# Layer one of a two-block network on Trainium2: 32x32 products apart from each other, ScalarE's U0 copy and the last pair's order moved

## The chip, the cores and the metric

The kernel runs on one core of one Trainium2 chip. A core has TensorE (PE in the profile, its weight loads are PEld), VectorE (DVE), ScalarE (ACT), GpSimd (POOL) and SyncE (SP), which here only issues DMAs. The metric is the device time of one execution in microseconds (us). It is read as the median of three runs.

## The reference

The program is a stack of four layers on 512 tokens of width 1024, each with a norm ahead and a residual sum behind. Layer one is the one that is changed. Its input projection gives nine parts; the part that matters here is a recurrent state per head:

```
z = h @ even_w_in[j]
a_val, a_glu, a_gate, r, k, v, wd, ad, b_gate = split_cols(z, EVEN_SIZES)
ya = conformer_conv(a_val, a_glu, ...) * silu(a_gate)      # 31 taps over time, per channel
yb = rwkv7_mix(r, k, v, wd, ad, ...) * silu(b_gate)
out = concatenate([ya, yb]) @ even_w_out[j]

def rwkv7_step(state, inp):            # 16 heads of 64, scanned over 512 tokens
    r_t, w_t, k_t, v_t, kk_t, a_t = inp
    sa = einsum('bhvk,bhk->bhv', state, -kk_t)
    state = state * w_t + sa[..., None] * (kk_t * a_t) + v_t[..., None] * k_t
    y = einsum('bhvk,bhk->bhv', state, r_t)
```

The other layers (sparse attention, a linear recurrence, attention with forget gates) are computed by code that the change does not touch.

## The kernel before

The 16 heads are worked off in eight pairs; a pair fills the 128 partitions. The scan over tokens is replaced by chunks of 64 tokens: in each chunk a triangular 64x64 system is solved, and a short chain carries the state from chunk to chunk. All eight chunks and both heads of a pair are handled at once.

To invert the triangular matrices, the kernel works on their 32x32 diagonal blocks with products of 32x32 matrices (`quarters`, line 1277; each set has 32 matmuls, which the trace shows as 64 records, for float32 runs in two passes). `sq1`, `sq2`, `sq3` square the matrix again and again; `sq2p`, `sq3p`, `sq4` multiply the powers into the running inverse `inner`; `off0`, `merge0`, `off1` and `merge1` join 16-blocks to 32-blocks and these to 64-blocks. Between two sets ScalarE copies the product out of PSUM (line 1883), VectorE transposes it (line 1647) or adds it to `inner` (line 1652). After `merge1` VectorE copies the result to `PT` (line 1665). Then come 64x64 products: `PAt`, `U0`, `PA`, `G`, `C`. `G` on TensorE needs VectorE's copy of `PAt` (line 1671); the second half of `C` needs ScalarE's copy of `U0` (line 1864). Six `chain` steps, `U`, `Y` and `y` end the pair.

The projections of the next pair are spread between these products. A projection has eight steps, `k0` to `k7`, then `r0` to `r7`, `v`, `glu`, `val`, `gate`. A step is three matmuls of 128x128 by 512 columns (lines 524, 525, 528), since each float32 weight is split into a rounded part `w_hi` (ScalarE, line 480) and a rest `w_lo` (GpSimd, line 498). Each is made in two halves of a block, and a step waits for the half that it reads. There are two split buffers and four raw ones. In them the labels `wk0`, `wk1`, `wr0` and so on are the halves for the block two places further on: `wk0` and `wk1` make v's weights, `wr0` and `wr1` glu's, `wv0` and `wv1` val's.

SyncE fetches the blocks in the order of a plan, each as soon as the block four places ahead of it has left its raw buffer (the loop from `weights_in`, line 441):

```
old = k.plan[n - NRAW] if n >= NRAW else None
free = None if old is None else ("rest_made", old[0], 1) if old[4] else ("modulated", old[0])
for w in need(free):
    e.wait_ge(*w)
e.dma_start(k.raw[n % NRAW][:, 0:kt * width], src)
```

Here NRAW is 4. Blocks of `ada` (for the modulation vectors) are not split; VectorE reads them once, in `ada0` to `ada3` (line 747), and so frees them. For each pair the plan is k, ada0, r, ada1, v, ada2, ada3, glu, val, gate.

VectorE fills its time with the 31 convolution taps of a channel block (`tap0` and so on, line 1599), which depend on nothing in the solve.

The order on each engine is written out by hand in three tables: `FIRST_ORDER` (ahead of and in the first pair), `ORDER` (for pairs in the middle) and `LAST_ORDER`. Every engine's streams are merged by the place of a label in its table. A `'` behind a label means one pair later, a `^` one period later in the first and last tables. Engines are in-order: an instruction that waits holds all that stands behind it.

In the last pair there is no next pair to project; its cover is the rest of the gates (`gate`, `cg`), the convolution norm's sums (`mean`, line 1459) and, on VectorE, the last 31 taps.

Of the kernel before, what the change touches and what calls it, by code (L numbers as in the profile page):

```python
# [3507 lines left out]
```

## Time and profile before

| what | value |
|---|---|
| median of 3 runs | 1765.78 us (1763.6 to 1766.76) |
| the profiled execution, its own time | 1764.11 us |
| span of its trace | 1762.4 us |
| mean granted clock of TensorE | 0.977 |
| PE, DVE, ACT, POOL busy | 1664.6, 1235.5, 806.0, 795.9 us |
| the eight pairs of layer one | about 88 to 620 us of the span |

Busy time is the sum over the whole span. Since the layers have different limits, what a change in the solve is worth is read from the solve's own stretches, engine by engine: a wait ahead of an instruction is shown in square brackets with what released it. The granted clock is in parts of 2.4 GHz; it is either 1.00 (2.4 GHz) or 0.50 (1.2 GHz), and means lie between.

### The profile page before, as it was taken

The numbers are of one execution on the slowest core, as the hardware profiler recorded it, in microseconds if no ns is written. First come the engines' busy times: TensorE is split into PE (matmuls) and PEld (weight loads), VectorE is DVE, ScalarE is ACT, GpSimd is POOL, SyncE is SP. The second block draws the span as 40 slices with busy tenths as digits, with TensorE's granted clock in tenths as the row PEclk, the third lists the DMA queues.
The fourth block names the chain that finished last, engine by engine and source line by source line (L and its number), as shares of the span: only waits on it lengthen the run. The fifth ranks groups of instructions, "written<-read, shape, count | busy, mean of one in ns | idle before, by whom it ended". The sixth has DMA issues, their size and how long they took to land.

```text
span 1762.4 us, 38758 instructions
## 1 busy us (share of the span) xinstructions
PE 1664.6 (94%) x16172; PEld 1267.4 (72%) x16172; DVE 1235.5 (70%) x2231; ACT 806.0 (46%) x1505; POOL 795.9 (45%) x713
## 2 busy tenths in 40 slices
PE   5899999999989899999999999999999999999997
PEld 5677776777776668757777777787777778777766
DVE  7578878988879788269997777535887436355553
ACT  3544444454443273365544444434767433444443
POOL 3534334344342245457883222544545545544433
PEclk9999999999999999999999999999999999999998
DMA  7212311312313123212221111123222232433312
GB/s 305 95 63 74 110 54 70 121 51 74 121 51 133 38 96 125 96 48 73 84 96 49 37 37 37 61 96 108 72 84 71 82 99 81 140 115 117 109 57 90
DMA packets 51902, 155.12 MB, mean 88 GB/s; under 512 B 5888, under 2 KB 12032, under 8 KB 51600
## 3 DMA queue, kind: packets, MB, share of 16 engines
q1 hardware_dynamic: 51728, 152.65, 25.6%
q8 instruction: 128, 2.10, 0.5%
q14 instruction: 46, 0.38, 0.1%
HBM read 150.50 MB, written 2.13 MB: 87 GB/s over the span
## 4 chain that ended last, share of the span: by engine, by line
PE 66%; DVE 20%; ACT 5%; issue 4%; POOL 2%; DVEq 0%; POOLq 0%; ACTq 0%
PE bank L524 16%; PE bank L528 14%; PE bank L525 14%; PE bank L1272 7%; PE bank L2360 3%; DVE ya L1599 2%; DVE best L2468 2%; DVE lru_xc L2852 2%; DVE score L2471 2%; PE bank L3077 1%; PE bank L1230 1%; PE bank L2390 1%; PE bank L3092 1%; DVE probs_t L2515 1%; PE bank L570 1%
## 5 line engine op out<-in xcount | busy, mean ns | idle before, releaser
L498 POOL TENSOR_TENSOR w_lo<-raw,w_hi 128x512 fp32r<-128x512 f32 (+2 forms) x434 | 578.6, 1349 | 603.2 <-ACT w_hi L480 591.7
L524 PE MATMUL bank<-h_hi,w_hi 128*128 128x512 f32 x1368 | 578.1, 423 | 10.2 <-ACT h_hi L973 2.5
L528 PE MATMUL bank<-h_lo,w_hi 128*128 128x512 f32 x1368 | 543.3, 397 | 10.8 <-DVE h_lo L941 6.3
L525 PE MATMUL bank<-h_hi,w_lo 128*128 128x512 f32 x1368 | 541.5, 396 | 0.0
L480 ACT ACTIVATE w_hi<-raw 128x512 fp32r<-128x512 f32 (+2 forms) x434 | 248.1, 603 | 252.7 <-PE bank L528 172.0
L524 PEld LDWEIGHTS bank<-h_hi,w_hi 128*128 128x128 f32 x1368 | 260.9, 191 | 100.2 <-issue 34.0
L528 PEld LDWEIGHTS bank<-h_lo,w_hi 128*128 128x128 f32 x1368 | 260.7, 191 | 77.1 <-DVE h_lo L941 11.4
L525 PEld LDWEIGHTS bank<-h_hi,w_lo 128*128 128x128 f32 x1368 | 261.5, 191 | 57.4 <-issue 9.3
L1599 DVE SCALAR_TENSOR_TENSOR ya<-padded,vecs,ya 128x512 f32<-128x512 f32 x240 | 214.2, 893 | 3.9
L3153 DVE CUSTOM_DVE_ANT_0 fox_probs<-bank,fox_keybias 128x128 f32<-128x128 f32 (+3 forms) x64 | 28.9, 488 | 84.7 <-PE bank L3077 84.4
L524 PE MATMUL bank<-own_hi,w_hi 128*128 128x512 f32 x208 | 82.9, 398 | 1.6 <-ACT own_hi L973 1.6
L528 PE MATMUL bank<-own_lo,w_hi 128*128 128x512 f32 x208 | 82.3, 396 | 0.0
L525 PE MATMUL bank<-own_hi,w_lo 128*128 128x512 f32 x208 | 82.0, 394 | 0.0
L3239 ACT ACTIVATE fox_probs<-fox_probs,fox_small 128x128 f32<-128x128 f32 (+3 forms) x64 | 35.5, 555 | 76.9 <-DVE fox_small L3159 76.9
L2360 PE MATMUL bank<-probs_t,values 32*128 32x256 f32 x1024 | 65.1, 394 | 5.1 <-DVE probs_t L2515 5.1
L2002 POOL TENSOR_TENSOR tables<-shifted_r 128x512 f32<-128x512 f32 x8 | 8.8, 1095 | 127.0 <-PE bank L528 127.0
L2360 PEld LDWEIGHTS bank<-probs_t,values 32*128 32x128 f32 x1024 | 50.7, 189 | 18.6 <-DVE probs_t L2515 8.5
L1883 ACT ACTIVATE W<-bank 128x256 f32<-128x256 f32 x32 | 12.3, 385 | 103.9 <-PE bank L1272 103.9
L1064 DVE SCALAR_TENSOR_TENSOR x<-bank,mod,x 128x512 f32<-128x512 f32 x16 | 12.0, 749 | 68.1 <-PE bank L528 68.1
L2555 ACT ACTIVATE attn_tmp<-bank 64x512 f32<-64x512 f32 (+1 forms) x54 | 31.9, 592 | 52.2 <-PE bank L528 48.7
L1062 DVE TENSOR_TENSOR x<-bank,x 128x512 f32<-128x512 f32 x16 | 11.1, 692 | 63.0 <-PE bank L528 63.0
L792 DVE TENSOR_TENSOR squares<-squares,sq 128x512 f32<-128x512 f32 x37 | 34.4, 942 | 27.1 <-ACT sq L782 26.5
(412 smaller groups left out, 2826.8 us busy)
## 6 DMA issues: line engine op xcount, KB each, us to landing
raw<-even_in SPq DMA_DIRECT2D x57, 512.0 KB, 3.7
raw<-odd_in SPq DMA_DIRECT2D x39, 512.0 KB, 3.2
raw<-ada SPq DMA_DIRECT2D x32, 512.0 KB, 4.0
raw<-fox_in SPq DMA_DIRECT2D x25, 512.0 KB, 3.3
raw<-lru_in SPq DMA_DIRECT2D x24, 512.0 KB, 3.2
ada_first<-ada SPq DMA_DIRECT2D x16, 512.0 KB, 13.7
raw<-even_out SPq DMA_DIRECT2D x16, 512.0 KB, 3.3
raw<-odd_out SPq DMA_DIRECT2D x16, 512.0 KB, 3.3
```

What stands on the lines that cost most here:

```text
L480: e.activation(k.w_hi[s % NSPLIT][:, at], k.raw[n % NRAW][:, at], ACT.Copy).then_inc(*did("rounded", key, half))
L498: e.tensor_tensor(k.w_lo[s % NSPLIT][:, at], k.raw[n % NRAW][:, at], k.w_hi[s % NSPLIT][:, at].bitcast(F32), ALU.subtract).then_inc(*did(" ...
L524: e.matmul(out, hi[:, w], x[i][0], start=start and i == 0, stop=False, skip_group_check=True)
L525: e.matmul(out, lo[:, w], x[i][0], start=False, stop=False, skip_group_check=True)
L528: m = e.matmul(out, hi[:, w], x[i][1], start=False, stop=stop and i == kt - 1, skip_group_check=True)
L1272: return e.matmul(out, lhsT, rhs, start=start, stop=stop, skip_group_check=True)
L1599: e.scalar_tensor_tensor(y, u[:, j:j + T], w(j), y, ALU.mult, ALU.add).then_inc(*did("tapped", q, j))
L2360: m = e.matmul(k.banks[3 + i][:, 0:GROUP * KB], k.values[rows, j, :], k.probs_t[n % 2][rows, j, :, :].rearrange("p a q -> p (a q)"), start ...
L2468: e.max(k.best[:, t - t0, :], k.score[:, t, :]).then_inc(*did("made", "best", t, n))
L2471: e.match_replace(k.score[:, t, :], k.best[:, t - t0, :], k.score[:, t, :], TAKEN).then_inc(*did("made", "taken", t, n))
L2852: e.scalar_tensor_tensor(xc, xp[:, j:j + T], w(j), xc, ALU.mult, ALU.add).then_inc(*did("made", *(("lru_tap", n, j) if j < LTAPS - 1 else ...
L3239: e.activation(prob, prob, ACT.Exp, bias=k.fox_small[:, 3 * i:3 * i + 1], scale=1.0, accum_out=k.fox_small[:, 3 * i + 1:3 * i + 2]).then_i ...
```

## The change

Only the tables change; all instructions are the same ones. In `ORDER`, and alike in `FIRST_ORDER` with `^` behind the labels:

```diff
-        gate7' k7 Z sq1 tK tB sq2 sq2p sq3 sq3p r0 r1 sq4 r2 r3 r4 off0 r5 r6 merge0 kk_sum r7 off1 v0 v1
-        v2 v3 merge1 v4 v5 v6 v7 PAt U0 PA G C glu0 glu1 chain1 ...
+        gate7' k7 Z sq1 tK tB r0 sq2 r1 r2 sq2p r3 sq3 r4 r5 sq3p r6 sq4 r7 v0 off0 v1 v2 merge0 kk_sum v3 off1
+        v4 v5 merge1 v6 v7 PAt U0 PA G C glu0 glu1 chain1 ...
```

VectorE's table in `ORDER` follows: it runs `... sq2 tap5 sq2p k_lerp tap6 sq3p f_out tap7 sq4 turn0 tap8 tap9 merge0 turn1 ada0 tap10 tap11 tap12 merge1 tap13 ada1 tap14 tap15 tap16 PAt ...`. On ScalarE `k_copy` comes ahead of `wk0`, `wk1` behind `sq3`, and `U0` ahead of `wr0 wr1 wv0`; on GpSimd `below` comes ahead of `wk0`. In `LAST_ORDER`:

```diff
-        gate7' gate0 gate1 gate2 gate3 gate4 gate5 gate6 gate7 cg00 sq2 sq2p sq3 sq3p mean2 mean3 mean4 mean5 mean6
-        sq4 cg01 cg02 cg03 cg04 cg05 off0 merge0 off1 cg06 cg07 cg10 ...
+        gate7' gate0 gate1 gate2 gate3 sq2 gate4 sq2p gate5 sq3 gate6 sq3p gate7 cg00 mean2 mean3 mean4 mean5 mean6
+        sq4 cg01 cg02 cg03 off0 cg04 cg05 merge0 cg06 off1 cg07 cg10 ...
-        tV ada0 mm0 mm1 N N_t val_done' tap25' ada1 ada2 ada3 f_norm tap26' tap27' tB tap28' tap29' tap30' sq1
+        tV ada0 mm0 mm1 N N_t val_done' tap25' sq1 tB ada1 ada2 f_norm tap26' tap27' tap28' tap29' tap30' ada3
```

and on ScalarE `gate_done` moves behind `sq3`.

TensorE's own order, in the first pair behind the transposes of K and B; the rows with `W` or `inner` are the sets `sq2` and `sq2p`, the others steps of r:

```order
 L1302 MATMUL bank<-ident,B_63 128x128 x4
+L524 MATMUL bank<-h_hi,w_hi_28 128x512
+L525 MATMUL bank<-h_hi,w_lo_30 128x512
+L528 MATMUL bank<-h_lo,w_hi_28 128x512
 L1272 MATMUL bank<-W_75 32x32 x32
+L524 MATMUL bank<-h_hi,w_hi_28 128x512
+L525 MATMUL bank<-h_hi,w_lo_30 128x512
+L528 MATMUL bank<-h_lo,w_hi_28 128x512
+L524 MATMUL bank<-h_hi,w_hi_28 128x512
+L525 MATMUL bank<-h_hi,w_lo_30 128x512
+L528 MATMUL bank<-h_lo,w_hi_28 128x512
 L1272 MATMUL bank<-inner,W_75 32x32 x32
```

One step now stands ahead of `sq2` and two between `sq2` and `sq2p`, where the sets followed each other.

VectorE's order in the first pair, around `merge1` (the copy to `PT`), `turn1` (the transpose of `inner` to `W_75`), `ada1` (L747 on `raw_24`) and the copy of `PAt` (to `W_77`):

```order
+L1599 SCALAR_TENSOR_TENSOR ya<-padded_87,vecs,ya 128x512 x3
+L1665 COPY PT<-bank 128x8x32
 L1599 SCALAR_TENSOR_TENSOR ya<-padded_87,vecs,ya 128x512
 L747 ISA raw_24,mod_11<-raw_24,silu_c 128x1024
 L747 ISA mod_11 128x1
 L752 TENSOR_TENSOR mod_11<-mod_11,vecs 128x1
-L1647 STREAM_TRANSPOSE W_75<-inner 128x256
-L1599 SCALAR_TENSOR_TENSOR ya<-padded_87,vecs,ya 128x512 x6
-L1665 COPY PT<-bank 128x8x32
-L1599 SCALAR_TENSOR_TENSOR ya<-padded_87,vecs,ya 128x512
+L1599 SCALAR_TENSOR_TENSOR ya<-padded_87,vecs,ya 128x512 x3
 L1671 COPY W_77<-bank 128x512
```

`ada1` stood ahead of `merge1` and now stands behind it, with three taps between it and the copy of `PAt`.

ScalarE's order in the first pair, from the end of `kk_root`; `W_75<-bank` is the copy of `U0`, `w_hi` are the roundings `wr0`, `wr1`, `wv0`:

```order
 L1794 ACTIVATE tables<-tables 128x512
 L1786 ACTIVATE shifted_r<-bank 128x512
+L1864 ACTIVATE W_75<-bank 128x512
 L480 ACTIVATE w_hi_28<-raw_24 128x512 x2
 L480 ACTIVATE w_hi_27<-raw_25 128x512
 L1786 ACTIVATE shifted_v<-bank 128x512
-L1864 ACTIVATE W_75<-bank 128x512
 L1910 ACTIVATE PA<-bank 128x256 x2
```

The copy of `U0` has moved from behind three roundings and `v_copy` to ahead of them.

## Rows read from the trace of the kernel before

**Rows 1.** The head of the page: busy time, share of the span, instructions.
```profile
PE 1664.6 (94%) x16172; PEld 1267.4 (72%) x16172; DVE 1235.5 (70%) x2231; ACT 806.0 (46%) x1505; POOL 795.9 (45%) x713
```
**Rows 2.** Stretches: length, busy PE, PEld, DVE, ACT, POOL; PEclk, DMA share, GB/s.
```profile
161.52:190.01 28.49, 26.27 (x846) 20.84 (x842) 22.41 (x38) 14.60 (x27) 8.82 (x7) 0.94 0.22 77
...
428.55:456.72 28.17, 26.20 (x846) 21.02 (x843) 22.48 (x39) 14.60 (x27) 8.84 (x7) 0.94 0.22 78
493.72:525.54 31.82, 27.33 (x846) 21.57 (x843) 22.39 (x38) 14.61 (x27) 9.23 (x8) 0.89 0.20 69
sum 208.79, PE 187.11 PEld 148.35 DVE 156.21 ACT 102.83 POOL 62.58; mean PE 26.73 PEld 21.19 DVE 22.32 ACT 14.69 POOL 8.94
```
**Rows 3.** Timeline of TensorE in the second pair: start, us, what, wait before.
```profile
163.33 0.71 PE L1272 MATMUL bank<-W 32*32 32x32 f32 x62
163.90 0.73 PE L1272 MATMUL bank<-inner,W 32*32 32x32 f32 x62
166.36 0.41 PE L1272 MATMUL bank<-W 32*32 32x32 f32 x27 [1.73 <-DVE W L1647]
168.43 0.80 PE L524 MATMUL bank<-h_hi,w_hi 128*128 128x512 f32 x1
171.29 0.75 PE L1272 MATMUL bank<-inner,W 32*32 32x32 f32 x64
174.25 0.75 PE L1272 MATMUL bank<-inner,W 32*32 32x32 f32 x64
176.52 0.75 PE L1272 MATMUL bank<-W 32*32 32x32 f32 x64
182.53 0.21 PE L1272 MATMUL bank<-W 32*32 32x32 f32 x1
186.15 1.15 PE L1272 MATMUL bank<-A_t,PT 64*64 64x64 f32 x32
188.47 0.22 PE L1272 MATMUL bank<-B_t,W 64*64 64x64 f32 x1
```
**Rows 4.** Two more stretches, columns as above, for the clock.
```profile
168.00:171.00 3.00, 3.00 (x42) 2.19 (x33) 2.43 (x4) 0.18 (x1) 1.35 (x2) 0.50 0.03 5
592.00:603.00 11.00, 8.50 (x255) 7.30 (x256) 9.54 (x16) 2.28 (x5) 1.28 (x1) 1.00 0.20 68
```
**Rows 5.** Timeline of VectorE in the second pair.
```profile
172.09 0.42 DVE L1652 TENSOR_TENSOR inner<-bank,inner 128x256 f32<-128x256 f32 x1 [0.80 <-PE bank L1272]
...
178.32 1.22 DVE L747 CUSTOM_DVE_ANT_0 raw<-raw,silu_c 128x1024 f32<-128x1024 f32 x1
...
180.02 4.65 DVE L1599 SCALAR_TENSOR_TENSOR ya<-padded,vecs,ya 128x512 f32<-128x512 f32 x6
...
187.35 0.69 DVE L1671 COPY W<-bank 128x512 f32<-128x512 f32 x1 [1.69 <-PE bank L1272]
```
**Rows 6.** Timelines of SyncE, ScalarE and GpSimd: fetches and splits of weights.
```profile
179.58 0.80 SPq L449 DMA_DIRECT2D raw<-even_in  x2
194.73 0.33 SPq L449 DMA_DIRECT2D raw<-even_in  x1
197.99 0.63 ACT L480 ACTIVATE w_hi<-raw 128x512 fp32r<-128x512 f32 x1 [8.03 <-DMA raw<-even_in]
186.09 1.66 ACT L480 ACTIVATE w_hi<-raw 128x512 fp32r<-128x512 f32 x3
187.27 2.96 POOL L498 TENSOR_TENSOR w_lo<-raw,w_hi 128x512 fp32r<-128x512 f32 x2
raw<-even_in SPq DMA_DIRECT2D x57, 512.0 KB, 3.7
```
**Rows 7.** Last pair: timelines of VectorE and TensorE.
```profile
569.41 0.44 DVE L1647 STREAM_TRANSPOSE W<-W 128x256 f32<-128x256 f32 x1
570.00 0.71 PE L1272 MATMUL bank<-W 32*32 32x32 f32 x62 [1.74 <-DVE W L1647]
596.52 0.68 PE L1272 MATMUL bank<-A_t,PT 64*64 64x64 f32 x16 [1.70 <-DVE PT L1665]
```

More of the change, by code:

```diff
@@ L1103 @@
         glu5 glu6 glu7 val0 val1 val2 val3 val4 val5 val6 val7 tA^ mm0^ bonus_sum tV^ k0^ w_up^ k1^ k2^ k3^ k4^ k5^
-        mm1^ N^ k6^ k7^ Z^ sq1^ tK^ tB^ sq2^ sq2p^ sq3^ sq3p^ r0^ r1^ sq4^ r2^ r3^ r4^ off0^ r5^ r6^ merge0^
-        kk_sum^ r7^ off1^ v0^ v1^ v2^ v3^ merge1^ v4^ v5^ v6^ v7^ PAt^ U0^ PA^ G^ C^ glu0^ glu1^ chain1^ glu2^
+        mm1^ N^ k6^ k7^ Z^ sq1^ tK^ tB^ r0^ sq2^ r1^ r2^ sq2p^ r3^ sq3^ r4^ r5^ sq3p^ r6^ sq4^ r7^ v0^ off0^ v1^ v2^
+        merge0^ kk_sum^ v3^ off1^ v4^ v5^ merge1^ v6^ v7^ PAt^ U0^ PA^ G^ C^ glu0^ glu1^ chain1^ glu2^
         chain2^ glu3^ chain3^ glu4^ glu5^ glu6^ glu7^ chain4^ val0^ val1^ chain5^ val2^ val3^ val4^ val5^ val6^
@@ L1109 @@
         cum powers carry k_lerp kk_norm A B r_lerp R rk v_lerp V mm0^ val_done tV^ tap0^ cum^ powers^ mm1^ N^ N_t^
-        carry^ tap1^ tap2^ sq1^ tap3^ tB^ tap4^ sq2^ sq2p^ k_lerp^ sq3p^ tap5^ sq4^ ada0^ tap6^ turn0^ tap7^ tap8^
-        merge0^ tap9^ ada1^ turn1^ tap10^ tap11^ tap12^ tap13^ tap14^ tap15^ merge1^ tap16^ PAt^ tap17^ G^ tap18^ C^
+        carry^ tap1^ tap2^ sq1^ tap3^ tB^ tap4^ sq2^ tap5^ sq2p^ k_lerp^ tap6^ sq3p^ tap7^ sq4^ turn0^ tap8^ tap9^
+        merge0^ turn1^ ada0^ tap10^ tap11^ tap12^ merge1^ tap13^ ada1^ tap14^ tap15^ tap16^ PAt^ tap17^ G^ tap18^ C^
         tap19^ chain1^ chain2^ ada2^ chain3^ kk_norm^ tap20^ ada3^ chain4^ A^ chain5^ B^ r_lerp^ chain6^ R^ U^ rk^
@@ L1128 @@
         mm0 val_done' tV tap0 tap25' cum tap26' tap27' powers tap28' tap29' f_norm mm1 N tap30' N_t carry tap1 tap2
-        sq1 tap3 tB tap4 sq2 sq2p k_lerp sq3p f_out tap5 sq4 ada0 tap6 turn0 tap7 tap8 merge0 tap9 ada1 turn1 tap10
-        tap11 tap12 tap13 tap14 tap15 merge1 tap16 PAt tap17 G tap18 C tap19 chain1 chain2 ada2 chain3 kk_norm tap20
+        sq1 tap3 tB tap4 sq2 tap5 sq2p k_lerp tap6 sq3p f_out tap7 sq4 turn0 tap8 tap9 merge0 turn1 ada0 tap10 tap11
+        tap12 merge1 tap13 ada1 tap14 tap15 tap16 PAt tap17 G tap18 C tap19 chain1 chain2 ada2 chain3 kk_norm tap20
         ada3 chain4 A chain5 B r_lerp chain6 R U rk v_lerp tap21 tap22 tap23 tap24 V""",
     "scalar": """
-        tA wval0' wval1' decay f_square f_log f_root powers wgate0' wgate1' before rate gate_done' N sq1 Z wk0 k_copy wk1 sq2
-        tK sq3 off0 kk_sq off1 kk_root r_copy wr0 wr1 wv0 v_copy U0 PA wv1 wglu0 V glu_done t1 wglu1""",
+        tA wval0' wval1' decay f_square f_log f_root powers wgate0' wgate1' before rate gate_done' N sq1 Z k_copy sq2 wk0
+        tK sq3 wk1 off0 kk_sq off1 kk_root r_copy U0 wr0 wr1 wv0 v_copy PA wv1 wglu0 V glu_done t1 wglu1""",
     "gpsimd": """
-        prior wgate0' inner wgate1' k_diff wk0 below wk1 r_diff wr0 wr1 wv0 wv1 v_diff wglu0 wglu1 wval0
+        prior wgate0' inner wgate1' k_diff below wk0 wk1 r_diff wr0 wr1 wv0 wv1 v_diff wglu0 wglu1 wval0
         wval1"""}
@@ L1156 @@
     "scalar": """
-        tA f_square f_log f_root wval0' wval1' N sq1 wgate0' Z tK wgate1' gate_done' gate_done sq2 sq3 off0 wgate0 wgate1
+        tA f_square f_log f_root wval0' wval1' N sq1 wgate0' Z tK wgate1' gate_done' sq2 sq3 gate_done off0 wgate0 wgate1
         wcg00 off1 cg_done0 wcg01 wcg10 wcg11 U0 PA cg_done1 cg_done2 centre0 centre1 t1 f_square^ centre2 centre3 centre4
```

12 lines of the change are left out of this document (6 added, 6 removed).

## The prediction

> **What bounds the kernel now.** I read the head of the page first. TensorE is busy for 94% of the span, so a gain must come from its idle time or from its clock, and it must reach TensorE [rows 1]. The change touches layer one, where eight head pairs are solved one after the other. For each of the first seven I took the stretch from the start of `sq1` to the first `glu` projection. It holds the same work in every pair and takes 28.17 to 31.82 us, 208.79 us in all seven. VectorE is busy in it for about 22.4 us, ScalarE for 14.6. The granted clock is the one number that separates them: mean 0.94 in three stretches (28.17 to 28.49 us), 0.89 in the other four, of which the longest takes 31.82 us [rows 2].
>
> The timeline of one pair says why. Between `sq2p` and `sq3` TensorE waits 1.73 us for a VectorE transpose. After that the clock is at 0.50, which is 1.2 GHz: the first projection after the sets starts at 168.43 and the next set only at 171.29, 2.86 us for two steps [rows 3, 4]. At 2.4 GHz a set with two steps takes 2.27 us (174.25 to 176.52) and a set with three 2.96 us (171.29 to 174.25). So **a step is 0.69 us, and a set that stands alone costs 0.89 us** with its edges [rows 3]. VectorE has nearly as much work. It waits 0.80 us at `sq4` and 1.69 at `PAt`, and taps fill the rest [rows 5].
>
> **Part one: the sets apart.** One or two r and v steps now stand between `sq2`, `sq2p`, `sq3`, `sq3p`, `sq4`. The copy and the transpose that `sq3` waits for take 0.38 to 0.45 us each, and two steps (1.37 us) and a set cover them; so the 1.73 us goes to nothing, and with it what precedes the low clock. The price is edges: back to back a set takes 0.57 us (163.33 to 163.90), alone 0.89, so three more groups cost about 1.0 us a pair [rows 3].
>
> The Trainium skill, "TensorEngine Tiling (Array Packing)", section Tiling Modes, says that changing the tiling mode drains TensorE. That speaks against every set put between 128-row projections. The trace agrees, and prices the drain together with the edges at the 0.3 us a set that I counted; by the rule alone the change would lose that and no more.
>
> Now the walk of one pair with these prices, from 163.3 where the transposes end. Up to `merge1` stand 14 steps (9.6 us), seven sets (6.2), `kk_sum` and the half set `off1` (about 0.85 each, from the like stretch after 176.52). `merge1` starts at 180.8 and `PAt`, two steps on, at 183.1; before they were at 182.53 and 186.15 [rows 3]. So TensorE is 3.0 us early at `PAt`. Were nothing else in the way, the stretch would shrink to 25.4 us (183.1 + 2.3 to `G` + 1.5 to the first `glu` step, less 161.5).
>
> **Part two: what is late next, VectorE.** The transpose `turn1`, both modulations and the taps change places. Between `merge1` and the copy of `PAt` VectorE used to have one tap; now it has a tap, `ada1` and three taps. The `merge1` copy starts 0.80 us after its set (171.29 to 172.09 shows this delay), at 181.6, and ends at 181.9; tap to 182.6; `ada1`, 1.22 us and 0.1 for its small followers, to 184.0; three taps of 0.78 (4.65 us for six) to 186.3; the copy of `PAt`, 0.69 us, to 187.0 [rows 3, 5]. `G` on TensorE needs it and would be ready at 183.1 + 2.3 = 185.4 (186.15 to 188.47 before). **TensorE waits 1.7 us ahead of G**, and `C` ends at 188.6. Behind the waiting `G` stand `C` and all the `glu` steps.
>
> **Part three: what is late after that, the weight ring.** This is where I put the bound. There are four raw buffers, and SyncE fetches in plan order: `glu`'s block takes the buffer that `ada1`'s block leaves. The trace shows it: `ada1` ends its pass at 179.54, and two even blocks (glu, val) are issued at 179.58 [rows 5, 6]. In the changed order `ada1` ends at 183.9, so `glu`'s block is issued 4.3 us later. From issue to the first rounding takes 3.3 us (194.73 to 197.99) to 3.7 (the page's median for such blocks): 187.4 or so. ScalarE rounds half a block in 0.6, GpSimd takes the rest in 1.3 to 1.7 (2.96 us for two), and each hand-over costs about 0.1 [rows 6]. That is 189.6 to 190.2, and I take 189.97. Before, GpSimd had the first half by about 188.8, out of the way. **So the first glu step starts 28.45 us after `sq1`** (ends 28.1 and 28.7), whatever TensorE gained earlier: 1.3 us of waiting stand behind `C`.
>
> Seven stretches are then 7 x 28.45 = 199.2 us against 208.79: **9.6 us less**. Nearly all of it is in the four pairs that had the clock at 0.89; the three others gain nothing.
>
> `U0` ahead of the roundings: its copy now comes where the roundings began before, at 186.09, and `C` needs it at about 188.0, so it hides; before, it sat behind three roundings (1.66 us) [rows 6]. It delays `glu`'s rounding only if that block had landed, which it has not. The GpSimd move (`below` before `wk0`) touches rows needed 5 us later. I cost both at nothing; with the ring out of the way that copy's 0.5 us or so (a third of 1.66) would show at `glu`.
>
> **The last pair.** VectorE comes to its `sq2` transpose at 569.41 without a wait ahead of it, so it is VectorE that is late, and `sq3` follows at 570.00 after 1.74 us [rows 7]. In the new order TensorE has only ten steps ahead of `sq3` where it had thirteen, and VectorE's `sq1` and `tB` come so early that each must wait for TensorE (I put 2 us on both, the 0.80 us delay above twice and a bit for the tap and copy that were cover). So `sq3` would be ready at about 567 and starts at about 571. The three steps come afterwards, partly in place of waits at `off0` and `merge0`. By this walk `merge0` is 1.7 us later: **plus 1.7 us** (0 to plus 4).
>
> **Sum.** The profiled execution took 1764.11 us (1762.4 of span and 1.7 around it). 1764.1 - 9.6 + 1.7 = 1756.2. The median of the three runs is 1.7 above the profiled one, so I forecast **1758 us**; within this case 1754 to 1762.
>
> **The rivals.**
>
> *A. Neither VectorE nor the ring limits.* VectorE catches up earlier in the pair, or the block lands before it is needed. For it: TensorE alone needs 25.4 us, and VectorE's 22.4 us of work fit into 27. The most that I can see is a stretch of 27.2 us, where `C` ends without the ring. That is 18.4 us less in seven; with the last pair's 1.7 back, 1749 us. Against it: the issue at 179.58 follows `ada1` to 0.1 us, so the ring is real.
>
> *B. The clock falls at the new waits, and the change loses.* Place: the 1.7 us ahead of `G` and the 1.3 us behind `C`, with 1.5 us of 64x64 products between. For it: in the pair of the timeline the clock fell after a wait of 1.73 us amid 32x32 products, and all seven stretches have a mean under 1.00 [rows 2 to 4]. Against it: in the last pair a wait of 1.70 us ahead of 64x64 products left the clock at 1.00 over the whole stretch around it [rows 4, 7]. Price: a mean of 0.94 over 28.17 us is 1.7 us lost; 0.89 over 31.82 us is 3.5 [rows 2]. It decides from about five pairs at 1.7: all seven give 1758 + 11.9 = 1770 us, slower than before; all at 3.5 would be 1782. Two or three pairs give 1762, no change.
>
> *C. The waits only move.* The edges, VectorE and the ring eat everything, with stretches of 29 us or more and a last pair at plus 4: 1764 to 1766 us.
>
> **How the numbers follow.** Forecast 0.45, A 0.15, B 0.28 (half of it in few pairs, half in most), C 0.12. Within 0.2% is 3.5 us, about what a measurement of this kernel can tell: 1762.3 to 1769.3. Faster takes the forecast nearly whole, less its upper edge, and A, with the best of B: 0.57. Same takes C and few pairs of B: 0.24. Slower takes the rest of B and a bad last pair: 0.19. The range from 1748 to 1770 leaves out the tails of A and B.
>
> **What would show it.** In the changed profile: no wait over 0.3 us between `sq1` and `merge1`, clock 1.00 there; `merge1` 19.3 us after `sq1`; a wait of 1 to 2 us ahead of `G` for the VectorE copy (L1671); two fetches issued right after `ada1`, 22.4 us after `sq1`; a wait ahead of the first `glu` step for GpSimd's w_lo (L498); all seven stretches alike. The forecast is wrong if the `glu` step starts without that wait (A), if the seven show clocks under 1.00 between `G` and `glu` (B), or if VectorE runs later than the walk has it ahead of `merge1`.

## The result, and the profile after

The change makes the kernel a little slower.

| kernel | median | lowest to highest | runs |
|---|---|---|---|
| before | 1763.87 us | 1759.02 to 1767.72 | 20 |
| after | 1768.01 us | 1764.30 to 1772.60 | 20 |

The ratio is 1.0024, 95% interval 1.0014 to 1.0033. I had forecast 1758 us and a gain. The time lies inside my range (1748 to 1770), the direction is wrong.

The profiled execution of after took 1772.13 us, with a span of 1770.4. That is at the upper edge of its own runs, so its trace shows some 4 us more than the kernel costs in the middle. The mean clock rose from 0.977 to 0.983. The head of the page of after (compare [rows 1]) shows that no engine has less or more work:

```profile
PE 1666.1 (94%) x16172; PEld 1262.3 (71%) x16172; DVE 1236.7 (70%) x2231; ACT 807.4 (46%) x1505; POOL 794.7 (45%) x713
```

The stretches from `sq1` to the first `glu` step in after, with the columns of [rows 2]:

```profile
160.75:190.54 29.79, 26.14 (x846) 19.87 (x843) 22.91 (x41) 13.73 (x25) 8.09 (x7) 1.00 0.20 74
227.91:260.07 32.16, 27.77 (x846) 21.50 (x843) 21.92 (x38) 14.81 (x27) 9.70 (x8) 0.95 0.20 68
...
367.42:395.59 28.17, 25.88 (x847) 19.71 (x843) 22.50 (x39) 13.47 (x24) 7.94 (x7) 1.00 0.22 79
...
sum 206.06, PE 184.04 PEld 140.32 DVE 157.20 ACT 96.66 POOL 57.86; mean PE 26.29 PEld 20.05 DVE 22.46 ACT 13.81 POOL 8.27
```

The clock is at 1.00 in six of the seven, where it was 0.94 or 0.89. The sum fell by 2.7 us only, from 208.79 to 206.06. The longest, the third, has a cause of its own, further below.

TensorE in the second pair of after, the same places as in [rows 3], and the wait at the end of the pair (this is `f_sum2`, line 1230):

```profile
173.18 0.74 PE L1272 MATMUL bank<-inner,W 32*32 32x32 f32 x62
174.88 0.24 PE L1272 MATMUL bank<-inner,W 32*32 32x32 f32 x2 [0.97 <-issue]
...
181.27 0.21 PE L1272 MATMUL bank<-W 32*32 32x32 f32 x1
...
187.38 0.61 PE L1272 MATMUL bank<-B_t,W 64*64 64x64 f32 x24 [0.83 <-DVE W L1671]
...
190.54 0.50 PE L524 MATMUL bank<-h_hi,w_hi 128*128 128x512 f32 x1 [1.62 <-POOL w_lo L498]
...
215.47 1.10 PE L1230 MATMUL bank<-post,head_ones 128*128 128x512 f32 x2 [0.62 <-ACT post L1850]
```

The waits that I forecast are there: 0.83 us ahead of `G` for VectorE's copy of `PAt`, 1.62 ahead of the first `glu` step for GpSimd's `w_lo`. Two are there that I had not: 0.97 us inside `off0`, with no releaser (what such pauses are is told in the last section), and 0.62 ahead of `f_sum2`, where it was 0.25 before.

VectorE in the same pair of after:

```profile
177.43 0.42 DVE L1652 TENSOR_TENSOR inner<-bank,inner 128x256 f32<-128x256 f32 x1 [2.65 <-PE bank L1272]
...
183.06 1.22 DVE L747 CUSTOM_DVE_ANT_0 raw<-raw,silu_c 128x1024 f32<-128x1024 f32 x1
...
184.40 2.32 DVE L1599 SCALAR_TENSOR_TENSOR ya<-padded,vecs,ya 128x512 f32<-128x512 f32 x3
186.64 0.68 DVE L1671 COPY W<-bank 128x512 f32<-128x512 f32 x1
...
192.51 0.28 DVE L1690 SCALAR_TENSOR_TENSOR S<-bank,carry,S 128x64 f32<-128x64 f32 x1 [1.48 <-PE bank L1272]
```

It waits 2.65 us at `merge0`, then is late at `PAt`'s copy (186.64, no wait ahead of it), and then waits again, 1.48 us at `chain1`, which stands behind the late `glu` steps.

SyncE, GpSimd and ScalarE of after, one fence each:

```profile
184.32 14.66 SPq L449 DMA_DIRECT2D raw<-even_in  x4
```

```profile
188.87 5.82 POOL L498 TENSOR_TENSOR w_lo<-raw,w_hi 128x512 fp32r<-128x512 f32 x4 [1.25 <-ACT w_hi L480]
```

```profile
188.16 1.91 ACT L480 ACTIVATE w_hi<-raw 128x512 fp32r<-128x512 f32 x3 [1.39 <-DMA raw<-even_in]
...
214.12 0.69 ACT L1803 ACTIVATE tables<-bank,half_bias 128x512 f32<-128x512 f32 x1 [2.60 <-DVE padded L1587]
```

The ring works as forecast: `ada1` ends its pass at 184.3, `glu`'s block is fetched at 184.32 and rounded at 188.16, after 1.39 us of waiting for it. The last row is the other end of the pair: ScalarE's `decay` waits for VectorE's `val_done` (line 1587), and `f_square` (line 1850), which `f_sum2` needs, is queued behind it.

The third pair of after, TensorE's timeline and two stretches (columns of [rows 2]):

```profile
254.04 1.28 PE L1272 MATMUL bank<-Z,PT 64*64 64x64 f32 x24 [1.74 <-issue]
...
259.69 0.46 PE L1272 MATMUL bank<-W,B_t 64*64 64x64 f32 x12 [1.61 <-issue]
```

```profile
254.40:257.80 3.40, 3.40 (x121) 3.40 (x119) 1.96 (x5) 1.65 (x4) 1.75 (x2) 0.50 0.49 159
261.20:268.00 6.80, 6.80 (x25) 4.01 (x24) 3.71 (x9) 0.00 (x0) 1.46 (x1) 0.50 0.16 39
```

Here 1.74 us pass inside `U0` and 1.61 inside the second half of `C`, both groups of 64x64 products, with no releaser in the profile, and behind each the clock is at 0.50, 1.2 GHz. This is close to rival B's place, in one pair of seven, but at other waits than the two that B named.

The last pair of after, VectorE, then TensorE, then a stretch for the clock (before: [rows 7]):

```profile
560.42 0.45 DVE L1647 STREAM_TRANSPOSE W<-W 128x256 f32<-128x256 f32 x1 [0.69 <-ACT W L1883]
562.10 0.69 DVE L1623 COPY B_t<-bank 128x512 f32<-128x512 f32 x1 [1.23 <-PE bank L1302]
562.71 2.01 DVE L747 CUSTOM_DVE_ANT_0 raw<-raw,silu_c 128x1024 f32<-128x1024 f32 x1
...
576.14 0.44 DVE L1647 STREAM_TRANSPOSE W<-W 128x256 f32<-128x256 f32 x1
```

```profile
576.73 1.08 PE L1272 MATMUL bank<-W 32*32 32x32 f32 x64 [6.03 <-DVE W L1647]
```

```profile
575.00:582.00 7.00, 5.27 (x135) 4.14 (x136) 6.27 (x11) 0.38 (x1) 0.00 (x0) 0.52 0.35 136
```

VectorE waits 1.92 us at `sq1` and `tB`, as I had put it (2 us). But TensorE now stands 6.03 us ahead of `sq3` (1.74 before), and then runs it and its neighbours at 1.2 GHz.

### The profile page after: what moved, and what is told of

The parts are those of the page before. It is cut to its first block, busy times and chain, and to the rows that moved or that the text cites. A ratio compares the mean times of both kernels' runs of the same rounds, so it can differ in the third digit from the quotient of the medians.

```text
span 1770.4 us, 38760 instructions
## 1 busy us (share of the span) xinstructions
PE 1666.1 (94%) x16172; PEld 1262.3 (71%) x16172; DVE 1236.7 (70%) x2231; ACT 807.4 (46%) x1505; POOL 794.7 (45%) x713
## 3 DMA queue, kind: packets, MB, share of 16 engines
q1 hardware_dynamic: 51728, 152.65, 25.4%
## 4 chain that ended last, share of the span: by engine, by line
PE 37%; DVE 13%; ACT 3%; issue 2%; POOL 1%; DVEq 0%; POOLq 0%; ACTq 0%
PE bank L524 8%; PE bank L528 8%; PE bank L525 8%; PE bank L2360 3%; DVE best L2468 2%; DVE score L2471 2%; DVE lru_xc L2852 2%; PE bank L3077 1%; PE bank L2390 1%; PE bank L3092 1%; DVE probs_t L2515 1%; PE bank L570 1%; DVE score L2455 1%; PE bank L572 1%; PE bank L571 1%
## 5 line engine op out<-in xcount | busy, mean ns | idle before, releaser
L528 PE MATMUL bank<-h_lo,w_hi 128*128 128x512 f32 x1368 | 541.8, 396 | 10.2 <-DVE h_lo L941 5.6
L1599 DVE SCALAR_TENSOR_TENSOR ya<-padded,vecs,ya 128x512 f32<-128x512 f32 x240 | 209.3, 872 | 3.6
L3153 DVE CUSTOM_DVE_ANT_0 fox_probs<-bank,fox_keybias 128x128 f32<-128x128 f32 (+3 forms) x64 | 28.9, 488 | 85.7 <-PE bank L3077 85.4
L3239 ACT ACTIVATE fox_probs<-fox_probs,fox_small 128x128 f32<-128x128 f32 (+3 forms) x64 | 35.5, 556 | 76.8 <-DVE fox_small L3159 76.8
L2360 PEld LDWEIGHTS bank<-probs_t,values 32*128 32x128 f32 x1024 | 49.7, 184 | 18.2 <-DVE probs_t L2515 8.5
L2002 POOL TENSOR_TENSOR tables<-shifted_r 128x512 f32<-128x512 f32 x8 | 10.9, 1359 | 110.0 <-ACT shifted_r L1786 110.0
```

The lines of the kernel that those rows point to most:

```text
L528: m = e.matmul(out, hi[:, w], x[i][1], start=False, stop=stop and i == kt - 1, skip_group_check=True)
L1599: e.scalar_tensor_tensor(y, u[:, j:j + T], w(j), y, ALU.mult, ALU.add).then_inc(*did("tapped", q, j))
L2360: m = e.matmul(k.banks[3 + i][:, 0:GROUP * KB], k.values[rows, j, :], k.probs_t[n % 2][rows, j, :, :].rearrange("p a q -> p (a q)"), start ...
L3239: e.activation(prob, prob, ACT.Exp, bias=k.fox_small[:, 3 * i:3 * i + 1], scale=1.0, accum_out=k.fox_small[:, 3 * i + 1:3 * i + 2]).then_i ...
```

## The experiments

Each was timed in five rounds beside the kernel before (4 to 11 executions of each); the ratio is to that kernel on the same chip. "Idle" is TensorE's time without work in seven periods, from the N products of the first pair to those of the last: the stretch less its busy time, as in these three rows (before, after, and the change without its last pair; columns of [rows 2]). It comes from one profiled execution of each kernel. Those of `e6_u0_only` (1769.6 us) and `e9_slots_filled` (1754.6) were the fastest of their kernels, 6.8 and 4.3 us below the median, so their idle times are not those of a typical execution.

```profile
90.49:549.96 459.47, 433.96 (x9079) 329.62 (x9072) 386.11 (x658) 205.58 (x364) 169.60 (x122) 0.96 0.24 82
```

```profile
90.50:554.11 463.61, 434.75 (x9077) 323.59 (x9071) 387.16 (x658) 206.92 (x364) 169.51 (x122) 0.99 0.23 81
```

```profile
91.59:552.58 460.99, 435.87 (x9078) 323.35 (x9072) 389.47 (x658) 207.65 (x365) 169.85 (x123) 0.99 0.23 81
```

| kernel | median us | ratio (95%) | idle us |
|---|---|---|---|
| before | 1763.4 to 1764.5 | 1 | 25.5 |
| after | 1768.0 | 1.0024 (1.0014 to 1.0033) | 28.9 |
| `e1_last_back` | 1762.7 | 0.9992 (0.9980 to 1.0004) | 25.1 |
| `e2_last_only` | 1769.6 | 1.0029 (1.0020 to 1.0038) | 25.9 |
| `e3_ada1_early` | 1762.7 | 0.9992 (0.9983 to 1.0000) | 23.3 |
| `e4_taps_moved` | 1789.8 | 1.0141 (1.0127 to 1.0155) | 43.6 |
| `e5_u0_back` | 1784.9 | 1.0112 (1.0099 to 1.0126) | 37.1 |
| `e6_u0_only` | 1776.4 | 1.0066 (1.0052 to 1.0080) | 35.5 |
| `e7_val_early` | 1759.8 | 0.9972 (0.9961 to 0.9983) | 21.5 |
| `e8_before_val_early` | 1762.8 | 0.9990 (0.9979 to 1.0002) | 25.4 |
| `e9_slots_filled` | 1758.9 | 0.9966 (0.9955 to 0.9977) | 20.2 |
| `e10_ring_early` | 1755.5 | 0.9957 (0.9945 to 0.9969) | 17.4 |
| `e11_rcopy_early` | 1757.0 | 0.9957 (0.9944 to 0.9970) | 18.2 |
| `e12_rounding_first` | 1751.1 | 0.9927 (0.9913 to 0.9940) | 12.6 |

### The last pair apart from the rest

`e1_last_back` is after with `LAST_ORDER` of before; `e2_last_only` is before with `LAST_ORDER` of after. The diff is the one shown with the change, cut in two.

> The changed kernel with the last pair's tables of before. Theory (the last pair pays): its VectorE order makes sq3 late, so this kernel is faster than the changed one by the 6.2 us that its profile lost between N and U of the last pair, or by 4 us at least: median ratio to before 0.998 to 1.001. In the last pair the wait of 6 us ahead of sq3 is gone and 1.7 us is back. Rival (the last pair's loss is absorbed by TensorE's later waits, as the prediction's walk had it): no more than 1.7 us faster than the changed kernel, ratio 1.0015 to 1.003.

> The kernel of before with the changed tables of the last pair alone. Theory (the last pair pays by itself): slower than before by 4 to 7 us, ratio 1.002 to 1.004, with a wait of about 6 us ahead of sq3 of the last pair. Rival (it pays only behind the other pairs' changes): within 2 us of before, ratio 0.999 to 1.001.

The last pair alone costs 0.29% (5.1 us); without it the change is worth nothing that can be measured (0.9992). The two effects add up to the whole, and both runs came out as expected. The seven stretches in `e1_last_back` take 199.31 us, against 199.2 in my walk. So the sum of the stretches was forecast to 0.1 us, and yet hardly anything of the 9.6 us reaches the time: the seven periods together grew from 459.5 to 461.0 us. TensorE's idle time in them is 25.5 us before and 25.1 here. **The waits have moved**: in the stretches they fell from 21.7 to 17.2 us, outside them they rose from 3.8 to 7.9.

What came back lies between the first `glu` step and the next pair's N products. The sums of these seven pieces, before and in `e1_last_back`, with the first pair's above each:

```profile
124.50:151.64 27.14, 26.83 (x303) 18.81 (x299) 25.46 (x44) 8.20 (x14) 10.52 (x8) 1.00 0.36 117
...
sum 187.53, PE 183.70 PEld 129.20 DVE 175.00 ACT 57.26 POOL 69.96; mean PE 26.24 PEld 18.46 DVE 25.00 ACT 8.18 POOL 9.99
```

```profile
124.01:155.25 31.24, 30.88 (x299) 21.33 (x300) 23.73 (x41) 9.42 (x18) 11.04 (x8) 0.85 0.31 102
...
sum 198.46, PE 190.58 PEld 132.91 DVE 177.91 ACT 69.30 POOL 77.56; mean PE 27.23 PEld 18.99 DVE 25.42 ACT 9.90 POOL 11.08
```

That is 10.9 us more, against 9.5 less in the stretches: 4.0 us are waits and 6.9 are busy time. Of the busy time 5.7 us come from two pieces in which the clock fell to 0.50: the first pair's (30.88 for 26.83 us) and the last piece, ahead of the last pair (24.46 for 22.86). So in this execution more than half of what came back is the clock. It shares the lowest mean clock of the kernel's eleven (0.983); the three at 0.988 and above took 1757.3 to 1761.0 us, though one at 0.987 took 1765.0. The other 1.2 us are about 0.3 in each of four pairs at clock 1.00, which I can't explain.

The sets' edges are not part of what came back, for all sets lie inside the stretches. Their price can be read from two stretches at clock 1.00, with the sets together (in `e8_before_val_early`) and apart (here):

```profile
161.04:188.40 27.36, 25.04 (x846) 19.98 (x843) 23.65 (x40) 14.60 (x27) 8.88 (x7) 1.00 0.22 80
```

```profile
365.41:393.21 27.80, 25.88 (x847) 19.71 (x843) 22.10 (x39) 12.90 (x23) 7.93 (x7) 1.00 0.22 80
```

That is 0.8 us of busy TensorE in this pair, and 0.8 to 1.1 in the other pairs of this kernel at clock 1.00, where I had counted 1.0.

### The ring and the taps behind it

`e3_ada1_early` and `e4_taps_moved` change VectorE's table of `e1_last_back`, and alike in `FIRST_ORDER`. The first diff is that of `e3_ada1_early`; the second comes on top of it in `e4_taps_moved` (cut at the dots, where the taps' numbers shift):

```diff
-turn1 ada0 tap10 tap11 tap12 merge1 tap13 ada1 tap14 tap15 tap16 PAt
+turn1 ada0 ada1 tap10 merge1 tap11 tap12 tap13 tap14 tap15 tap16 PAt
```

```diff
-k_lerp tap6 sq3p f_out tap7 sq4 turn0 tap8 tap9 merge0 ... PAt tap17 G ... v_lerp tap21
+k_lerp tap6 tap7 tap8 sq3p f_out sq4 turn0 tap9 tap10 tap11 merge0 ... PAt tap14 G ... v_lerp tap19 tap20 tap21
```

> As e1, and VectorE runs ada1 right behind ada0, two taps later in its place, so that the work between merge1 and the copy of PAt stays the same (six taps of 4.65 us for a tap, ada1 and three taps of 4.4). Theory (the weight ring): the fetch of glu's block comes about 3 us earlier, the wait ahead of the first glu step (0.9 to 1.6 us) is gone, the wait ahead of G stays at about 1 us; each of seven stretches is 1 to 1.5 us shorter, in all 7 to 10 us faster than e1. Rival (VectorE's lateness alone counts, the fetch was only close behind it): less than 2 us faster than e1.

> As e3, and VectorE's taps are moved out of the place between merge1 and the copy of PAt: two more stand in its idle time ahead of sq3p, one ahead of merge0, one by each of G, C and the chain, and two behind v_lerp. Theory (VectorE late at PAt, then the ring): both waits are gone, the stretch from sq1 to the first glu step comes to 27 us in each of seven pairs, 5 us or more below e3 in all and 10 to 15 below before: ratio 0.992 to 0.996. Rival (the work only moves: VectorE is the bound of the whole pair): the stretch is short but the time comes back behind it, at V, mm and val, ratio within 0.001 of e3's.

In the first, the wait ahead of `glu` goes and the one ahead of `G` grows from 0.84 to 2.01 us, on six taps in a row; the total stays at 0.9992, where I had expected 7 to 10 us less:

```profile
189.57 0.61 PE L1272 MATMUL bank<-B_t,W 64*64 64x64 f32 x24 [2.01 <-DVE W L1671]
```

Behind this wait the clock is at 0.50 for 3.4 us in four of the seven pairs, as rival B had it.

The second has the shortest stretches so far (197.1 us) and is 26 us slower than before, where I had expected a gain (0.992 to 0.996). Two more taps stand behind `v_lerp` (six for four), and each pair now waits for it at `f_sum2`, in this row of TensorE's timeline:

```profile
224.59 1.94 PE L1230 MATMUL bank<-post,head_ones 128*128 128x512 f32 x2 [4.26 <-ACT post L1850]
```

That row gave me the theory for the rest, L: from `PAt`'s copy to the next pair's `val_done` VectorE works nearly without a pause (27.1 to 27.6 us in pairs two to six of `e1_last_back`, 1.1 to 2.3 of them idle; 25.8 to 26.1 before), `val_done` releases ScalarE's `decay` and `f_square`, and these release `f_sum2`. What comes late out of the solve stays late to the end of the pair.

### Two taps past `val_done`

`e7_val_early` makes this edit in `e1_last_back`, `e8_before_val_early` in the kernel before (`LAST_ORDER` gets `tap23' tap24'` ahead of `tap25'`):

```diff
-mm0 val_done' tV tap0 tap25' cum tap26' tap27' powers tap28' tap29' f_norm mm1 N tap30' N_t carry
+mm0 val_done' tV tap0 tap23' cum tap24' tap25' powers tap26' tap27' f_norm mm1 N tap28' N_t tap29' tap30' carry
...
-v_lerp tap21 tap22 tap23 tap24 V
+v_lerp tap21 tap22 V
```

> The first-and-middle part of the change with the last pair's tables of before, and two of the four taps that VectorE does behind v_lerp moved past val_done of the next turn, into its wait of 2.5 us behind N. Theory L: from PAt's copy to val_done VectorE works 24 us nearly without a wait, and val_done releases ScalarE's decay and f_square and with it the f_sum2 product (0.30, 0.63, 0.86, 0.84, 0.86, 0.86 and 0.94 us of TensorE's waiting, 5.3 us in seven pairs). Two taps are 1.5 us, so all of these waits go: about 1758 us, ratio 0.996. Rival E (the edges of the sets and the clock have eaten the gain, VectorE's lateness is cover only): no change, 1762 to 1763; the wait comes back at N or sq1.

> The kernel before with the same move of two taps past val_done, nothing of the change. The waits at f_sum2 are 0.26, 0.25, 0.25, 0.45, 0.46, 0.25 and 1.4 us there (3.3 in all, of which the last has another releaser): Theory L gives up to 1.9 us less, ratio 0.999, so that the move is worth about 3 us more in the changed kernel than here. Rival E: the same small effect in both. A third: VectorE's later taps behind N push sq1's or sq2p's transposes, and it is slower by a microsecond or two.

The same two taps are worth 3.5 us in the changed kernel (0.9992 to 0.9972, intervals that overlap by 0.0003) and 1.7 or less in the old one (0.9990, not told from nothing). In both traces the waits at `f_sum2` are gone in the first six pairs. Theory L holds in direction; the size is a little less than the 4.4 us of waits that the move takes away there.

### U0's place on ScalarE

I had costed this part of the change at nothing. `e5_u0_back` takes it out of `e1_last_back`, `e6_u0_only` puts it alone into the kernel before:

```diff
-r_copy wr0 wr1 wv0 v_copy U0 PA
+r_copy U0 wr0 wr1 wv0 v_copy PA
```

(as written for `e6_u0_only`; the other way round for `e5_u0_back`, in both tables).

> The first-and-middle part of the change with the last pair's tables of before, and ScalarE's copy of U0 back behind three roundings. Theory L (the time comes back behind the sets through VectorE): U0 has nothing to do with it; C needs the copy 1.9 us after PAt's, the roundings ahead of it are about 1.7 us, so TensorE waits at C no more than 0.3 us longer and that only moves the wait of 0.8 to 1.6 us ahead of the first glu step: 1762.7 us, ratio to the kernel before 0.999, within 0.1% of the same kernel with U0 ahead. Rival M (the moved copy is itself a cost, since it keeps the wv roundings, and so VectorE's and GpSimd's turn, back): 1759 to 1761, and the wait ahead of the first glu step falls below 0.5 us in most pairs.

> The kernel before with ScalarE's copy of U0 ahead of wr0, wr1 and wv0, nothing else of the change. In the changed tables this place is worth 22 us, for the roundings there wait 1.9 us for glu's block. In the kernel before the block has landed when ScalarE comes to it, so theory L says that the copy had 1.7 us of slack and the move is worth nothing: within 0.1% of the kernel before. A rival: ScalarE's roundings half a microsecond later delay GpSimd and so the first glu step: 1766 us, plus 0.1 to 0.2%.

Both of my expectations were wrong, and by much. The four combinations:

| | sets as before | sets apart |
|---|---|---|
| U0 behind the roundings | 1 | 1.0112 |
| U0 ahead of them | 1.0066 | 0.9992 |

In `e5_u0_back` ScalarE stands at `glu`'s rounding, whose block has not landed, and U0's copy is queued behind it; TensorE waits 3.11 us in the midst of `C`, and 22.1 us there in seven pairs (ScalarE, then TensorE):

```profile
191.84 1.91 ACT L480 ACTIVATE w_hi<-raw 128x512 fp32r<-128x512 f32 x3 [1.89 <-DMA raw<-even_in]
...
194.13 0.59 ACT L1864 ACTIVATE W<-bank 128x512 f32<-128x512 f32 x1
```

```profile
194.77 1.01 PE L1272 MATMUL bank<-V_t,K_t 64*64 64x64 f32 x25 [3.11 <-ACT W L1864]
```

In `e6_u0_only` it is the reverse. The block is there, but U0's product is not, and the roundings are queued behind the waiting copy:

```profile
188.30 0.60 ACT L1864 ACTIVATE W<-bank 128x512 f32<-128x512 f32 x1 [2.12 <-PE bank L1272]
188.79 1.66 ACT L480 ACTIVATE w_hi<-raw 128x512 fp32r<-128x512 f32 x3
```

```profile
190.82 0.50 PE L524 MATMUL bank<-h_hi,w_hi 128*128 128x512 f32 x1 [0.71 <-POOL w_lo L498]
...
216.24 1.10 PE L1230 MATMUL bank<-post,head_ones 128*128 128x512 f32 x2 [0.87 <-ACT post L1850]
```

Rounding starts 36.4 us after the pair's N products (152.41), where it was 34.5 (186.09 less 151.64, [rows 6]). The first row's wait is what `glu` pays at once; the second shows the same lateness once more at the end of the pair. So the order of the two is right only for one order of their inputs, and the change moved the inputs too: counted from the pair's N products (151.64 before, 150.86 after), TensorE comes to `PAt` and `U0` 1.8 us earlier (183.54 for 186.15) and the block is issued 5.5 us later (184.32 for 179.58).

### Filling VectorE's waits

With theory L the cure is to take out VectorE's own waits, so that it is not late behind the solve. `e9_slots_filled` and `e10_ring_early` both keep the edit of `e7_val_early` and write VectorE's middle anew (first line: changed kernel):

```diff
-k_lerp tap6 sq3p f_out tap7 sq4 turn0 tap8 tap9 merge0 turn1 ada0 tap10 tap11 tap12 merge1 tap13 ada1 tap14 tap15 tap16 PAt
+k_lerp tap6 tap7 sq3p f_out tap8 sq4 turn0 tap9 tap10 tap11 merge0 turn1 ada0 ada1 tap12 merge1 tap13 tap14 PAt
+k_lerp tap6 ada0 sq3p f_out tap7 sq4 turn0 tap8 tap9 ada1 merge0 turn1 tap10 tap11 tap12 tap13 merge1 tap14 tap15 PAt
```

> As the kernel with two taps past val_done and the changed sets, and besides that VectorE's waits ahead of sq3p (2.0 us) and merge0 (1.4 to 2.6) take one more tap each, both modulations stand ahead of the merge1 copy (so glu's block is fetched earlier), two taps instead of four stand between it and PAt's copy. Theory L: the waits ahead of G (0.8 to 1.0), ahead of glu (0.7 to 1.6) and at f_sum2 (0.3 to 0.9) all go, some 2.5 us a pair: down to 1748, ratio 0.991. Rival E: TensorE has the work and the edges, so what is left is the 0.3 to 0.9 us inside the sets, and no more than 5 us is gained: 1757. Rival B (the clock): the last waits have moved onto 64x64 products and 3.4 us at 1.2 GHz appear in the pairs, 1.7 us each: 1755 to 1762.

> As the kernel with the slots filled (1758.9 us), but ada0 takes VectorE's wait ahead of sq3p and ada1 that ahead of merge0, about 3 us earlier, and the tap ahead of ada3 goes back behind it. In the former the first glu step still waits 0.8 to 1.5 us for GpSimd's w_lo and chain4 0.9 to 1.1 us for VectorE. If the ring is what limits glu, glu's block lands by 377 of that pair's clock and that wait falls to 0.5 (GpSimd's r_diff and ScalarE's U0 are then last), and the one at chain4 to nothing: 1.5 us a pair, 1748 us, ratio 0.991. If the edges and the clock set the pair, 1757 to 1759, no change, and the time shows as waits or low clock elsewhere. If ada0 or ada1 make sq3p, sq4 or merge0 late, sets wait for VectorE again and the time is over 1760.

> As the kernel with ada0 and ada1 in VectorE's waits, and ScalarE's r_copy ahead of off1's copy instead of behind kk_root, 9 us earlier, in a stretch where ScalarE waits 3.7 us for TensorE. GpSimd's r_diff (1.04 us) then lies before the first rounding, and U0's copy and the roundings come 0.5 us earlier. If after the ring GpSimd is last ahead of glu, this takes what is left of that wait: 0.5 to 1 us a pair, 3 to 6 us in seven, ratio 0.989. If the block is still what is waited for, no difference between the two.

`e9_slots_filled` gains only 1 us more (0.9966 for 0.9972, not told apart). `glu` still waits 0.8 to 1.5 us in three pairs and 0.2 in a fourth, and `chain4` 0.5 to 1.1 in all for VectorE, since I had put two taps ahead of `ada3`. `e10_ring_early` shortens both, to 0.7 us at `glu` in six pairs and 0.5 or less at `chain4`, and gives 0.9957: 8 us below the kernel before, where I had expected 16. `e11_rcopy_early` turned out to be the same instructions in the same order as `e10_ring_early`: in the code `r_copy` follows `kk_root` in one stream, so a label placed ahead moves nothing. It is a second reading of that kernel (0.9957 both times) and no test of its edit.

`e12_rounding_first` makes that edit in earnest, in `prepare`, and puts `wr0` ahead of `U0`:

```diff
-        yield at["kk_root"]
-        ready(("multiplied", "kk_sum", q))
-        inverse_root(sq, q)
         yield at["r_copy"]
         copy("r", q, even_key("r", q), ...)
+        yield at["kk_root"]
+        ready(("multiplied", "kk_sum", q))
+        inverse_root(sq, q)
...
-kk_sq off1 kk_root r_copy U0 wr0 wr1 wv0
+kk_sq r_copy off1 kk_root wr0 U0 wr1 wv0
```

> As the kernel with ada0 and ada1 in VectorE's waits (1755.5 us), with two edits on ScalarE: r_copy really ahead of off1's copy (its instruction is moved in the code too, since the label alone moved nothing in the run before: that one was the same program again), and wr0, the first half of glu's rounding, ahead of U0's copy. In that kernel the block has landed when ScalarE comes to it, and the first glu step waits 0.71 us in nearly every pair for GpSimd's w_lo, which follows r_diff (379.77 to 380.8) and the rounding (from 380.1). If those two are what is last ahead of glu, w_lo starts a microsecond earlier and the wait goes: up to 5 us less in seven pairs, 1751 us, ratio 0.993. If the pair is bound by TensorE's own work and by the 0.3 to 1.6 us inside the sets, the wait goes and comes back elsewhere: 1755 to 1757. If r_copy, queued ahead of off1's copy, or U0's copy half a microsecond later holds TensorE, over 1758.

1751.1 us, ratio 0.9927: better than both kernels, and what was expected to the microsecond. Which of the two edits the gain belongs to was not tried. ScalarE, GpSimd and TensorE in the fifth pair:

```profile
377.55 0.61 ACT L480 ACTIVATE w_hi<-raw 128x512 fp32r<-128x512 f32 x1
378.07 0.58 ACT L1864 ACTIVATE W<-bank 128x512 f32<-128x512 f32 x1
```

```profile
378.24 6.41 POOL L498 TENSOR_TENSOR w_lo<-raw,w_hi 128x512 fp32r<-128x512 f32 x4 [8.26 <-ACT w_hi L480]
```

```profile
379.79 0.50 PE L524 MATMUL bank<-h_hi,w_hi 128*128 128x512 f32 x1
```

`glu`'s first step has no wait ahead of it in any of the seven pairs. Of the 12.6 us of idle time that are left 5.9 are of another kind, a pause inside a set without a releaser, as here in the second pair:

```profile
173.25 0.24 PE L1272 MATMUL bank<-inner,W 32*32 32x32 f32 x2 [1.83 <-issue]
```

## Why the prediction was wrong

**What bounds the kernel now.** I read the clock rightly. The wait for VectorE inside the sets I took from one pair's timeline; in the others a good part of it has no releaser. I took the stretch from `sq1` to `glu` as the thing to sum and stopped there. The waits at `f_sum2`, 0.25 to 0.46 us before, are small, so I did not see that VectorE has no slack from `PAt`'s copy on.

**Part one, the sets apart.** Right in kind. The waits for VectorE between the sets went and the clock there is 1.00 in six stretches of seven. `merge1` came 20.5 us after `sq1` in the second pair, not 19.3; 0.97 of it is the wait with no releaser. Such pauses make up 13.9 us of the idle time in the sets before, which I had put down to VectorE, and 7.3 are still there after. TensorE waits in them for its own instructions (last section), so a part of what the steps between the sets gave was time for those, which the prediction did not have. The edges cost 0.8 to 1.1 us a pair, as I had counted.

**Part two, VectorE.** Right in kind: VectorE is late at `PAt`'s copy and `G` waits for it. The copy ended at 187.3 (walk 187.0), but `sq1` had started 0.8 us earlier than in the walk; counted from `sq1` that is 26.6 us for 25.5, so the close time is luck. The wait ahead of `G` is 0.8 to 1.0 us where I had 1.7.

**Part three, the weight ring.** Right in kind: `glu`'s block follows `ada1`, and `glu` waits for it through `w_lo`. The sum is right to a tenth in the kernel without its last pair, 199.31 us against 199.2, and that is in part luck. The pair that I walked took 29.27 us, not 28.45, and others as little as 27.80. The changed kernel, which has the same instructions in the same order in these pairs, took 206.06 in its profiled execution; 5.7 of the 6.7 us between the two are pauses without a releaser (7.3 against 1.6).

**The step that failed** is the next one, in the sum: "1764.1 - 9.6 + 1.7". It takes the 9.6 us out of the stretches for 9.6 us out of the kernel. `e1_last_back` gives 1.3 us of them. Rival C, "the waits only move", was this case, and I had priced it only inside the stretch. Between the stretches 10.9 us came back: 4.0 of waits and 6.9 of busy time, 5.7 of it where the clock was at 0.50. I had taken this part of a pair as unchanged. `e7_val_early` shows one of the paths, VectorE's taps ahead of `val_done`, worth 3.5 us. How the rest divides I have from one profiled execution, not from a timed experiment, and no run here sets the clock apart.

**`U0`, costed at nothing.** Wrong. With the sets apart its place is worth 1.2% (1.0112 against 0.9992). My sentence said that the block had not landed and that the copy therefore delays no rounding. That same fact means that in the old order the copy would wait for the block, and I did not turn the sentence round.

**The last pair, plus 1.7 us.** Mis-sized: 5 us (`e1_last_back`, `e2_last_only`). The two waits on VectorE were right (1.92 us). I let TensorE start `sq3` at 571. In the trace it starts at 576.73, with the N products of that pair at 554.11 instead of 549.96, so 2.6 us later in the pair. What I left out is that the cover in front of `sq3` was taken away while VectorE came no earlier. TensorE then stands for 6.03 us, and works at 1.2 GHz behind it for almost 7 us, the three moved steps included, where it had 3.4 us at that clock before.

**Rival B** happened in one pair of after, and in the first of `e1_last_back`, where 10.2 us at 1.2 GHz begin within the 1.62 us ahead of `glu`. It also came behind the 2.06 us ahead of `G` in four pairs of `e3_ada1_early`. Other pairs with the same waits kept 2.4 GHz. In after it is not what makes the kernel slower, for the last pair's 5 us do that; of the gain that did not arrive in `e1_last_back` it is the largest part that the trace shows (5.7 of 10.9 us).

## What to carry to other kernels

A stretch that gets shorter is a gain only if the engines come out of it earlier; take the sum over a whole period, and look at TensorE's idle time and at its clock in all of it before and after. When two instructions on an in-order engine wait for different things, their order is right or wrong by which input comes first, so a change that moves the inputs has to be walked again at each such pair. Cover taken from ahead of a wait costs the wait in full unless what it waits for comes earlier too.

## What was not expected of the hardware

**VectorE and GpSimd.** VectorE's passes over `ada`'s blocks take longer when GpSimd splits weights at the same time. In the groups of instructions of the seven pairs (count, busy us, mean ns) before and in `e1_last_back`:

```profile
L747 DVE CUSTOM_DVE_ANT_0 raw<-raw,silu_c 128x1024 f32<-128x1024 f32 x28 | 34.7, 1240 | 0.0
```

```profile
L747 DVE CUSTOM_DVE_ANT_0 raw<-raw,silu_c 128x1024 f32<-128x1024 f32 x28 | 40.1, 1434 | 0.0
```

That is 5.4 us more in seven pairs, since `w_lo` now runs into `ada2`: in the fifth pair of after GpSimd works until 400.16 (394.26 and 5.90), and `ada2`, which starts at 398.90, takes 2.34 us. The Trainium skill, "SBUF — State Buffer", section SBUF: two separate sides, says that VectorE with two SBUF inputs and a GpSimd operation that reads SBUF lock each other out for a whole instruction; the trace agrees, the pass ends 1.08 us behind GpSimd and takes 1.22 when alone. `ada2` lies on VectorE's path from `PAt`'s copy to `val_done`, so these 1.1 us are a part of the lateness at `f_sum2` in `e1_last_back`; no run here takes them away alone.

**Waits without a releaser: TensorE's own instructions.** TensorE pauses within one set of products, and the profile names no releaser. In after and in `e12_rounding_first` most of these pauses stand at the same instruction: after 62 of 64 records in the second pair (0.97 and 1.83 us), after 53 in the fourth (0.89 and 1.25), after 58 in the sixth (0.69 and 1.92). They add up to 7.3 us in seven pairs of after, 1.6 in `e1_last_back`, whose instructions there are the same, 5.9 in `e12_rounding_first` and 13.9 before, where the longest takes 2.34 us (fourth pair, within an `inner,W` set).

Counting TensorE's instructions in the trace (each matmul, each weight load and the few of its sequencer), every pause over 0.15 us without a releaser, 116 in the fourteen traces of this case, stands at number 193 or 194 of a block of 256. The page of after has a DMA queue that carries instructions:

```profile
q8 instruction: 128, 2.10, 0.5%
```

All its 128 packets are 16,384 bytes each, and 128 times 256 is 32,768, where the trace has 32,901 instructions of TensorE. Each of the 116 pauses ends 1.2 to 1.6 us after such a packet has ended: in the second pair of after the packet ends at 173.52 and TensorE goes on at 174.88, in the third pair before at 234.22 and 235.58. At none of the other block edges does TensorE come closer than 1.2 us behind the packet. So TensorE waits here for its own instructions. The sets use them fastest: two sets one behind the other are 128 matmul records with their weight loads, a whole block, in 1.1 us (0.57 each), while one packet takes 0.9 to 1.8 us in this layer. That fits the fall from 13.9 us to 7.3 and 1.6 once the sets stand apart. Why the same place costs 0.47 us in one execution and 1.83 in another is open, and no run was made to change the fetch.

**Fetches queued together.** In `e9_slots_filled` `glu`'s block is issued 1.3 us behind two `ada` blocks, at 374.94, and rounded only at 381.30, 6.36 us later; at 184.32 in after, with no fetch just ahead of it, this took 3.84 us.
